# A hybrid decoder step on one core: entry products of 344 columns, the sticks' bias added ahead, w_out loaded early, and a combine that gathers with addition

## The chip, the core and the metric

The kernel is one program on one NeuronCore of a Trainium2 chip. The time is device microseconds from the start to the end of an execution. Five engines work in parallel, each on its own instruction stream: PE (TensorE, matrix products), DVE (VectorE), ACT (ScalarE), POOL (GpSimd) and SP (SyncE, which here only issues transfers). Sixteen DMA engines move data between HBM and the on-chip memory. Products land in eight PSUM banks; everything else on the chip lies in one large SBUF allocation that the kernel calls the arena, beside the activations h (token rows) and hT (transposed).

## The reference

One inference step of a one-layer hybrid trunk, for a prompt of 1024 tokens and a sample group of 8 sequences with 4 tokens each; the model width is 1024, all numbers are float32.

```python
h = layer_norm(x, ln0)
z = h @ w_in                      # split: qa ka va | ub vb | xc | qkv | zg | bd ad
# A stick-breaking attention, 4 heads of 64
z = q @ k.T * dh**-0.5 + bias
log_beta, log_keep = log_sigmoid(z), where(mask, log_sigmoid(-z), 0)
after = exclusive reverse cumulative sum of log_keep over the keys
oa = where(mask, exp(log_beta + after), 0) @ v
# B chunked gated MLP, C causal pooling of windows 2/4/8/16, D gated delta rule in chunks of 64
h = layer_norm(ALPHA * h + concat(oa, ob, oc, od) @ w_out, ln1)
h = layer_norm(ALPHA * h + cross_attention(h, mem_k, mem_v), ln2)   # mem_k = mem_prompt @ xa_wk
# 16 experts in 4 groups, the best two of the best group, gates g1, g2
h = layer_norm(ALPHA * h + g1 * expert1(h) + g2 * expert2(h), ln3)
```

The sample group runs through the same weights with cached keys, values and states. The outputs are the two streams and all new caches and states.

## The kernel before

The program is a row of fourteen stages, each in one block at whose end all engines join. Within a stage each engine runs its instructions in the order in which they are written, and semaphores order the engines against each other. There is no scheduler: the order in the code is the order on the engine. Tokens lie in nine tiles, eight of 128 prompt tokens and one of the 32 sample tokens (`TILES`, `rows(i)`). A float32 product is recorded as two matmul instructions. The places that the change touches:

**Entry** (`stage_entry`, lines 302 to 494). DVE normalises tile after tile, PE transposes it (L455) and multiplies it by the first part of w_in (L471): two products of 512 columns (keys and values; gate values and pooling input) and one of 8 columns (the delta gates), each over eight parts of the depth. ACT copies the four quarters out of the banks, DVE the 8 columns. SP issues the eight x tiles, the weights behind x tile 1, and stores h, k and v per tile.

**Sticks** (`stage_stick_prompt`, 881 to 1078). Eight query blocks of 128; block qb attends to qb+1 key blocks, the diagonal one first: 36 steps. A step n is: scores(n) on PE (L957), add_bias(n) on DVE (L1039), softplus(n) in three activations on ACT (L1009 to L1011), soft_sum(n) on DVE (L1047, and L1050 for the mask on a diagonal), suffix(n) on PE (L967, and L971 off the diagonal), argument(n) on DVE (L1056), weights(n) on ACT (L1017), values(n) on PE (L987). In an iteration n of the loops PE runs scores(n), suffix(n-1), values(n-2); ACT weights(n-2), softplus(n); DVE argument(n-2), soft_sum(n-1), add_bias(n). The waits that matter: add_bias(n) for the four products of scores(n), suffix(n-1) for soft_sum(n-1), argument(n-2) for suffix(n-2).

**Sample** (`stage_sample_and_inputs`, 1081 to 1372): the sample's attention over the cached pages (keys transposed by PE, `turn`, L1165 on), the delta rule's gates and decays (L1178), and the norms of its queries, keys and values, all in one order per engine.

**Delta and residual** (`stage_delta`, 1374 on; `stage_residual`, 2115 on, run twice, for w_out with tag "o" and for xa_wo with tag "w"). SP reloads h in the delta stage and loads w_out at the residual's start in four pieces (L2151). ACT rounds each piece to a high part (L2258), DVE makes the low part (L2231), PE multiplies in three passes (L2110 to L2112), DVE adds to h (L2211).

**Memory** (`stage_memory`, 2283 on): PE transposes mem_prompt (L2326) and multiplies by xa_wk and xa_wv (L2340); SP issues all of it at the stage's start.

**Route and experts** (`stage_route`, 2707 on; `stage_experts`, 2911 on): the route makes for every row of an expert's tile the token that it reads, by one-hot products (L2772). The experts' hidden product is a DVE multiply.

**Combine** (`stage_combine`, 3161 to 3250): POOL gathers the two expert rows of every token into a ring of six buffers (L3193), DVE multiplies each by its gate and adds it to h (L3219) and takes statistics (L283 to L285), ACT normalises (L3250), DVE multiplies by the gain (L3229), POOL adds the shift (L3206), SP stores.

Of the kernel before, what the change touches and what calls it, by code (L numbers as in the profile page):

```python
# [176 lines left out]
def setup(nc, ctx, T, O):  # L177
# [86 lines left out]
    c.gate, c.off = small(2 * TILES), small(2)  # L264
# [37 lines left out]
def stage_entry(c):  # L302
# [28 lines left out]
    w_in, const_in, ln_in = s("e_w"), s("e_const"), s("e_ln")  # L331
    eps_set, stats, rstd_ok, normed = s("e_eps"), s("e_stats"), s("e_rstd"), s("e_normed")
    turned, hT_ok, proj_kv, proj_vx, proj_ba = s("e_turned"), s("e_hT"), s("e_kv"), s("e_vx"), s("e_ba")
    kv_out, vx_out, ba_out, k_turned, kT_ok = s("e_kvo"), s("e_vxo"), s("e_bao"), s("e_kt"), s("e_kTo")
    stored = [s("e_stored0"), s("e_stored1")]
    dve_chain, act_chain, zeroed = s("e_dve"), s("e_act"), s("e_zero")
    w_view = T['w_in'][0].rearrange("(k p) n -> p k n", p=P)

    with nc.Block() as block:
        @block.sync  # L340
        def _(sp):
            for i in range(TILES):
# [11 lines left out]
            for i in range(TILES):  # L354
                sp.wait_ge(normed, i + 1)
                sp.dma_start(c.tokens_dram[i * P:i * P + rows(i), :], h[0:rows(i), i, :]).then_inc(h_out, 16)
                sp.wait_ge(kv_out, 2 * i + 2)
# [13 lines left out]
        def _(dve):  # L371
# [6 lines left out]
            def evac_ba(i):  # L378
                dve.wait_ge(proj_ba, i + 1)
                nc.vector.tensor_copy(c.ba[0:rows(i), i, :], ps[4][0:rows(i), 0:8]).then_inc(ba_out, 1)  # L380

            for i in range(TILES):
# [9 lines left out]
                if i >= 2:  # L392
                    evac_ba(i - 2)
            evac_ba(TILES - 2)
            evac_ba(TILES - 1)

        @block.scalar
        def _(act):
# [6 lines left out]
            def evac(i):  # L405
                r = rows(i)
                act.wait_ge(proj_kv, i + 1)
# [3 lines left out]
                nc.scalar.copy(ktok[0:r, i % 2, :], ps[2 + 4 * (i % 2)][0:r, 0:256]).then_inc(kv_out, 1)  # L411
                nc.scalar.copy(vtok[0:r, i, :], ps[2 + 4 * (i % 2)][0:r, 256:512]).then_inc(kv_out, 1)
                act.wait_ge(proj_vx, i + 1)
                nc.scalar.copy(vg[0:r, i, :], ps[3 + 4 * (i % 2)][0:r, 0:256]).then_inc(vx_out, 1)
                nc.scalar.copy(xc[0:r, i, :], ps[3 + 4 * (i % 2)][0:r, 256:512]).then_inc(vx_out, 1)
# [14 lines left out]
            for i in range(TILES + 2):  # L430
# [8 lines left out]
                if 1 <= i <= TILES:  # L439
# [5 lines left out]
        def _(pe):  # L445
# [13 lines left out]
            def project(i):  # L459
                r = rows(i)  # L460
# [2850 lines left out]
```

## Time and profile before

| | |
|---|---|
| median of 3 runs | 1683.14 us (1682.97 to 1685.85) |
| profiled execution, its span | 1684.2 us, 1682.4 us |
| mean granted clock of TensorE | 0.908 of 2.4 GHz |
| busy: PE, DVE, ACT, POOL | 1386.1, 747.3, 448.1, 207.7 us |
| moved | 174.30 MB, mean 104 GB/s |

The stages by the trace (from join to join, read from busy time per window):

| stage | from, to us | PE busy | DVE | ACT | clock |
|---|---|---|---|---|---|
| entry | 0, 174.8 | 152.1 | 44.0 | 28.8 | 1.00 |
| features, gate and pool | 174.8, 364.0 | 167.7 | 85.4 | 63.1 | 0.94, 0.78 |
| sticks | 364.0, 500.8 | 113.7 | 87.1 | 91.3 | 0.94 |
| sample and inputs | 500.8, 535.5 | 25.1 | 20.9 | 19.6 | 0.85 |
| delta | 535.5, 702.0 | 141.9 | 89.6 | 51.4 | 0.85 |
| residual "o" | 702.0, 827.0 | 108.5 | 82.4 | 30.3 | 0.92 |
| memory | 827.0, 902.7 | 62.7 | 5.5 | 4.4 | 0.88 |
| queries, cross | 902.7, 1112.0 | 193.1 | 45.9 | 61.7 | 0.96, 0.98 |
| residual "w" | 1112.0, 1235.9 | 108.0 | 72.6 | 30.3 | 0.95 |
| route | 1235.9, 1289.4 | 23.5 | 27.8 | 2.9 | 0.66 |
| experts | 1289.4, 1606.8 | 289.8 | 126.2 | 43.0 | 0.96 |
| combine | 1606.8, 1682.4 | 0.0 | 59.9 | 21.4 | 0.50 |

The stages follow one another, so their lengths add up to the span. A busy share says how full an engine is in a stage, not what ends it. The clock column is what the chip granted to TensorE: 1.00 is 2.4 GHz and 0.50 is 1.2 GHz. Profiled time and span differ by the 1.8 us that lie around the span.

### The profile page before, as it was taken

How to read it: one execution, taken by the hardware profiler on the slowest of the kernel's cores; microseconds unless marked ns; L12 is line 12 of the kernel's file. 1: busy time of each engine (PE TensorE's matmuls, PEld its weight loads, DVE VectorE, ACT ScalarE, POOL GpSimd, SP SyncE). 2: the span in 40 equal slices, each digit the busy share in tenths (PEclk: the TensorE clock that was granted, in tenths of full speed). 3: DMA queues.
4: the chain of work that ended last, by engine and by line, in shares of the span. 5: the costliest groups of instructions: out<-in, count | busy, mean ns of one | idle time of the engine just before them, and what ended most of it. 6: DMA issues, size and time to landing. Idle time of an engine off the chain costs nothing. (4 is left out here: it accounts for less than half of the span.)

```text
span 1682.4 us, 24853 instructions
## 1 busy us (share of the span) xinstructions
PE 1386.1 (82%) x9807; PEld 936.7 (56%) x9808; DVE 747.3 (44%) x1132; ACT 448.1 (27%) x928; POOL 207.7 (12%) x196
## 2 busy tenths in 40 slices
PE   4999899778886997699698998969961998999900
PEld 2554799654444787488446987858821333333300
DVE  3321545237655564576401003346535443444368
ACT  1111424236765332322101214431110111111122
POOL 0000000003332751000000000000000110111056
PEclk9999899879997998599798999989985999999955
DMA  8110111022002100300351115430054495772153
GB/s 316 38 57 30 34 49 51 18 76 57 1 1 93 29 4 4 117 22 1 115 185 38 38 50 194 157 133 1 1 237 192 157 360 211 275 295 99 51 220 139
DMA packets 76946, 174.30 MB, mean 104 GB/s; under 512 B 12932, under 2 KB 40715, under 8 KB 70435
## 3 DMA queue, kind: packets, MB, share of 16 engines
q1 hardware_dynamic: 67387, 137.73, 23.2%
q0 software_dynamic: 5856, 21.24, 3.7%
q10 hardware_dynamic: 3600, 13.90, 2.0%
q8 instruction: 73, 1.20, 0.3%
q14 instruction: 30, 0.25, 0.0%
HBM read 142.27 MB, written 30.66 MB: 103 GB/s over the span
## 5 line engine op out<-in xcount | busy, mean ns | idle before, releaser
L2997 PE MATMUL bank<-arena,hT 128*64 x384 | 173.7, 606 | 11.3 <-DVE hT L3106 4.9
L2998 PE MATMUL bank<-arena,hT 128*64 128x512 f32 x384 | 173.7, 606 | 0.0
L471 PE MATMUL bank<-arena,hT 128*128 128x512 f32 (+3 forms) x432 | 141.1, 481 | 0.0
L2997 PEld LDWEIGHTS bank<-arena,hT 128*64 128x64 f32 x384 | 53.5, 140 | 124.2 <-issue 124.2
L3116 DVE COPY arena<-arena 128x4096 f32 x24 | 55.1, 2295 | 131.3 <-PE bank L2998 119.3
L471 PEld LDWEIGHTS bank<-arena,hT 128*128 128x128 f32 (+1 forms) x432 | 68.5, 184 | 72.8 <-issue 72.8
L2965 POOL DMA_INDIRECT hT<-tokens,row_token x24 | 40.3, 1678 | 440.4 <-PE bank L2982 229.8
L2111 PE MATMUL bank<-hT_rest,f_w_high 128*128 128x352 f32 x288 | 93.7, 326 | 0.0
L3021 PE MATMUL bank<-arena,hT 128*64 x192 | 87.5, 598 | 2.4 <-ACT hT L3061 2.4
L3023 PE MATMUL bank<-arena,hT 128*64 128x512 f32 x192 | 87.5, 598 | 0.0
L1577 PE MATMUL bank<-arena 64*64 64x64 f32 (+1 forms) x1920 | 68.6, 224 | 3.5 <-DVE arena L1950 3.0
L1577 PEld LDWEIGHTS bank<-arena 64*64 64x64 f32 x1920 | 64.2, 136 | 11.0 <-issue 6.5
L2110 PE MATMUL bank<-hT_high,q_w_high 128*128 128x352 f32 x192 | 62.6, 326 | 7.6 <-DVE q_w_low L2401 7.6
L2110 PE MATMUL bank<-o_w_high,o_s_high 128*128 128x512 f32 (+1 forms) x144 | 57.6, 400 | 12.6 <-DVE o_w_low L2231 12.6
L2110 PE MATMUL bank<-w_w_high,w_s_high 128*128 128x512 f32 (+1 forms) x144 | 57.5, 399 | 10.6 <-DVE w_w_low L2231 10.6
L2110 PE MATMUL bank<-f_h_high_a,f_w_high 128*128 128x352 f32 x180 | 59.2, 329 | 6.6 <-DVE f_w_low L668 6.6
L3061 ACT COPY hT<-bank 128x256 f32<-128x256 f32 x24 | 8.9, 373 | 204.6 <-PE bank L3009 202.3
L2112 PE MATMUL bank<-hT_high,q_w_low 128*128 128x352 f32 x192 | 63.3, 329 | 0.0
L2111 PE MATMUL bank<-hT_low,q_w_high 128*128 128x352 f32 x192 | 63.0, 328 | 0.0
L967 PE MATMUL bank<-arena,const 128*128 128x512 f32 x72 | 42.7, 677 | 21.4 <-DVE arena L1050 11.8
L2340 PE MATMUL bank<-arena 128*128 128x512 f32 x128 | 57.2, 609 | 2.0 <-DMA arena<-in_xa_wk_dram 2.0
L2112 PE MATMUL bank<-f_h_high_a,f_w_low 128*128 128x352 f32 x180 | 58.8, 327 | 0.0
(484 smaller groups left out, 2979.3 us busy)
## 6 DMA issues: line engine op xcount, KB each, us to landing
arena<-in_ex_wg_dram SPq DMA_DIRECT2D x16, 1024.0 KB, 7.5
arena<-in_ex_wu_dram SPq DMA_DIRECT2D x16, 1024.0 KB, 10.2
arena<-in_ex_wd_dram SPq DMA_DIRECT2D x16, 1024.0 KB, 12.3
expert_rows<-hT ACTq DMA_DIRECT2D x24, 512.0 KB, 5.2
arena<-in_cache_mem_k_dram SPq DMA_DIRECT2D x8, 1024.0 KB, 4.9
arena<-in_w_in_dram SPq DMA_DIRECT2D x12, 512.0 KB, 3.9
h<-in_x_prompt_dram SPq DMA_DIRECT2D x8, 512.0 KB, 8.9
arena<-in_w_in_dram SPq DMA_DIRECT2D x2, 2048.0 KB, 17.1
```

Of the source, the lines that this page charges most:

```text
L471: last = nc.tensor.matmul(ps[bank][0:r, 0:n], hT[:, k, i * P:i * P + r], wt[:, k, col:col + n], start=(k == 0), stop=(k == KC - 1))
L967: last = nc.tensor.matmul(ps[4 + n % 2][:, :], K("negsuf"), sp_[:, n % 3].rearrange(flat), start=True, stop=(kb == qb))
L1577: last = nc.tensor.matmul(out(q, hd), stationary(q, hd), moving(q, hd), start=True, stop=True)
L2110: nc.tensor.matmul(out, high, w_high, start=start, stop=False)
L2111: nc.tensor.matmul(out, high, w_low, start=False, stop=False)
L2112: return nc.tensor.matmul(out, low, w_high, start=False, stop=stop)
L2340: last = nc.tensor.matmul(ps[4 + u % 4][:, :], memT[:, k, m * P:(m + 1) * P], w[:, half % 3, k, :], start=(k == 0), stop=(k == KC - 1))
L2997: nc.tensor.matmul(ps[UPB[u % 2]][0:LR, :], xT[:, u % 2, k, 0:LR], gate_up_of[:, bass.ds(slot, 1), :, k, :].rearrange("p a g f -> p (a g) ...
L2998: last = nc.tensor.matmul(ps[UPB[u % 2]][LR:P, :], xT[:, u % 2, k, LR:P], wB_gate_up[:, :, k, :], start=(k == 0), stop=(k == KC - 1))
L3021: nc.tensor.matmul(ps[DNB[q]][0:LR, :], hidT[:, u % 2, f, 0:LR], down_of[:, bass.ds(slot, 1), f, n].rearrange("p a n -> p (a n)"), start=( ...
L3023: last = nc.tensor.matmul(ps[DNB[q]][LR:P, :], hidT[:, u % 2, f, LR:P], wB_down[:, f, n], start=(f == 0), stop=(f == 1))
L3116: nc.vector.tensor_copy(wB[:, 0:2 * EW], c.xw[:, bass.ds(e & 3, 1), 0:2 * EW].rearrange("p a n -> p (a n)")).then_inc(copied_up, 1)
```

## The change

Six edits, in the order of the program.

Entry: the 1032 columns of the weights are cut into three products of 344 columns instead of 512, 512 and 8. They rotate through five banks. The weights come in these thirds, and the first of them is issued in front of x tile 1. ACT copies the first two thirds, DVE the last. The sample tile is computed as four products of 256 or 264 columns that stand side by side in four groups of 32 columns of the array, and DVE copies all of it.

```diff
+    W3 = 344
+    THIRDS = (((0, KA, W3),), ((W3, KA + W3, 512 - W3), (512, VB, 2 * W3 - 512)), ((2 * W3, VB + 2 * W3 - 512, 1024 - 2 * W3), (1024, BD, 8)))
+    BANKS = (2, 3, 4, 6, 7)
...
-                if i == 1:
-                    sp.dma_start(wt[:, :, 0:512], w_view[:, :, KA:KA + 512]).then_inc(w_in, 16)
-                    sp.dma_start(wt[:, :, 512:1024], w_view[:, :, VB:VB + 512]).then_inc(w_in, 16)
-                    sp.dma_start(wt[:, :, 1024:1032], w_view[:, :, BD:BD + 8]).then_inc(w_in, 16)
+                if i < 2:
+                    for n in ((0,), (1, 2))[i]:
+                        for at, col, w in THIRDS[n]:
+                            sp.dma_start(wt[:, :, at:at + w], w_view[:, :, col:col + w]).then_inc(w_in[n], 16)
...
+                    for k in range(KC):
+                        last = nc.tensor.matmul(bank_of(i, n)[:, 0:W3], hT[:, k, t], wt[:, k, n * W3:(n + 1) * W3],
+                                                start=(k == 0), stop=(k == KC - 1))
+                    last.then_inc(third[n], 1)
+
+            def project_sample():
+                pe.wait_ge(hT_ok, 2 * NT + 2)
+                pe.wait_ge(vg_out, NT - 1)
+                for k in range(KC):
+                    for j in range(4):
+                        n = 264 if j == 3 else 256
+                        last = nc.tensor.matmul(bank_of(NT, 0)[j * NS:(j + 1) * NS, 0:n], hT[:, k, SEQ:TOK],
+                                                wt[:, k, j * 256:j * 256 + n], start=(k == 0), stop=(k == KC - 1))
```

The transfers that SP issues at the program's start, before:

```order
L343 DMA h<-in_x_prompt_dram 128x1024
L345 DMA arena<-in_ln_g_dram 128x1024
L346 DMA arena<-in_ln_b_dram 128x1024
L343 DMA h<-in_x_prompt_dram 128x1024
L348 DMA arena<-in_w_in_dram 128x8x512
L349 DMA arena<-in_w_in_dram 128x8x512
L350 DMA arena<-in_w_in_dram 128x8x8
```

The same place of the changed kernel (x tiles are L349 there, the weights L356):

```order
L349 DMA h<-in_x_prompt_dram 128x1024
L351 DMA arena<-in_ln_g_dram 128x1024
L352 DMA arena<-in_ln_b_dram 128x1024
L356 DMA arena<-in_w_in_dram 128x8x344
L349 DMA h<-in_x_prompt_dram 128x1024
L356 DMA arena<-in_w_in_dram 128x8x168
L356 DMA arena<-in_w_in_dram 128x8x176
L356 DMA arena<-in_w_in_dram 128x8x336
L356 DMA arena<-in_w_in_dram 128x8x8
```

The first 344 columns of the weights have moved in front of the second x tile; the other columns stay behind it.

Sticks: in DVE's loop add_bias(n) stands before argument(n-2) and soft_sum(n-1), and no longer behind them. PE's and ACT's loops are as they were.

```diff
             for n in range(N + 3):
                 if n >= 3 and steps[n - 3][0] == steps[n - 3][1]:
                     mask_weights(n - 3)
+                if n < N:
+                    add_bias(n)
                 if 2 <= n <= N + 1:
                     argument(n - 2)
                 if 1 <= n <= N:
                     soft_sum(n - 1)
-                if n < N:
-                    add_bias(n)
```

DVE in the sticks stage around the end of a query block, before (L1065 copies a block's output, L1061 is the mask on the weights, L1056 argument, L1047 soft_sum, L1039 add_bias):

```order
L1065 COPY hT<-bank 128x2x128 [waits a_pv]
L1061 TENSOR_TENSOR arena<-arena,const 128x512 [waits a_exp]
L1056 TENSOR_TENSOR arena<-bank,arena 128x512 [waits a_sp,a_sums]
L1047 SCALAR_TENSOR_TENSOR arena<-arena 128x512 [waits a_sumok,a_sums,a_soft]
L1039 TENSOR_TENSOR arena<-bank,arena 128x512 [waits a_exp,a_score]
L1056 TENSOR_TENSOR arena<-bank,arena 128x512 [waits a_sp,a_sums]
```

And in the changed kernel (L1102, L1098, L1076 add_bias, L1093 argument, L1084 soft_sum):

```order
L1102 COPY hT<-bank 128x2x128 [waits a_pv]
L1098 TENSOR_TENSOR arena<-arena,const 128x512 [waits a_exp]
L1076 TENSOR_TENSOR arena<-bank,arena 128x512 [waits a_exp,a_score]
L1093 TENSOR_TENSOR arena<-bank,arena 128x512 [waits a_sp,a_sums]
L1084 SCALAR_TENSOR_TENSOR arena<-arena 128x512 [waits a_sumok,a_sums,a_soft]
L1076 TENSOR_TENSOR arena<-bank,arena 128x512 [waits a_exp,a_score]
```

The operation that waits for the scores (a_score) is now the first of a step's three; the other two keep their order.

Sample: PE begins with the first square sums, transposes the keys of all eight sequences in one run, then does the second square sums and the decays (in bank 4 instead of 5); the order of ACT and DVE follows, and one memset goes from DVE to POOL.

```diff
+            square_sums(0)
             pe.wait_ge(c.k_pages_in, 16 * NPAGES)
-            for b in range(4):
+            for b in range(DB):
                 turn(b)
+            square_sums(1)
             decays()
-            for b in range(4, DB):
-                turn(b)
-            square_sums(0)
             pe.wait_ge(q_ok, 3)
```

Delta, residual and memory: the delta stage no longer reloads h; SP loads w_out into h's place there. The residual takes w_out from it, and h's tiles are loaded when the fourth low part is made. At the residual's end, behind the last product, SP issues the memory tensor and the first half of xa_wk.

```diff
-            sp.dma_start(c.h[:, 0:NT, :], c.tokens_dram[0:SEQ, :].rearrange("(i p) d -> p i d", p=P)).then_inc(sx["hin"], 16)
-            sp.dma_start(c.h[0:NS, NT, :], c.tokens_dram[SEQ:TOK, :]).then_inc(sx["hin"], 16)
+            load_w_out(c, sp)
...
+            if split:
+                sp.wait_ge(wl_ok, 4)
+                for i in range(TILES):
+                    sp.dma_start(h[0:rows(i), i, :], c.tokens_dram[i * P:i * P + rows(i), :]).then_inc(h_in[i], 16)
             c.clear_semaphores(sp)
+            if split:
+                sp.wait_ge(prod, 2 * TILES)
+                load_memory_first(c, sp)
...
+def load_w_out(c, sp):
+
+    wv = c.T['w_out'][0].rearrange("(k p) n -> p k n", p=P)
+    raw = c.h[:, 0:KC, :]
+    for n in range(4):
+        sp.dma_start(w_piece(raw, n), w_piece(wv, n)).then_inc(c.w_out_in[n], 16)
```

Route and experts: the one-hot products carry a second set of 24 columns, each entry times the token's gate, so that every row of an expert's tile has its gate (`row_gate`), and the experts' hidden product multiplies by it.

```diff
+                ins = vt.tensor_tensor(x[:, :, 1, :], x[:, :, 1, :],
+                                       c.gate[:, q * TILES:(q + 1) * TILES].unsqueeze(2).to_broadcast([P, TILES, NL]), ALU.mult)
...
+            link(vt.tensor_copy(c.row_gate, ps[3][:, MOE_TILES:2 * MOE_TILES]))
...
-                nc.vector.tensor_tensor(hid[:, u % 2, :], ps[UPB[u % 2]][:, DE:2 * DE], sg[:, u % 2, :], ALU.mult).then_inc(hid_ok, 1)
+                nc.vector.scalar_tensor_tensor(hid[:, u % 2, :], ps[UPB[u % 2]][:, DE:2 * DE], c.row_gate[:, bass.ds(t, 1)],
+                                               sg[:, u % 2, :], ALU.mult, ALU.mult).then_inc(hid_ok, 1)
```

Combine: the first gather of a tile adds its rows into h on the way, the second goes into its own buffer; none waits. DVE adds the second, takes statistics, and applies mean, gain, reciprocal deviation and shift in two instructions. ACT computes the reciprocal deviation only.

```diff
             for i in range(TILES):
-                for n in (S + 2 * i, S + 2 * i + 1):
-                    if n < 2 * TILES:
-                        gather(n)
                 r = rows(i)
-                gp.wait_ge(gained, i + 1)
-                nc.gpsimd.tensor_tensor(h[0:r, i, :], h[0:r, i, :], b[0:r, :], ALU.add).then_inc(normed, 1)
+                gp.indirect_dma_start(h[0:r, i, :], None, expert_rows, rows_of(i, 0), compute_op=ALU.add).then_inc(added[i], 16)
+                gp.indirect_dma_start(second[0:r, i, :], None, expert_rows, rows_of(i, 1)).then_inc(second_in[i], 16)
...
+            def measure(i):
+                r = rows(i)
+                dve.wait_ge(added[i], 16)
+                dve.wait_ge(second_in[i], 16)
+                nc.vector.tensor_tensor(h[0:r, i, :], h[0:r, i, :], second[0:r, i, :], ALU.add).then_inc(summed, 1)
...
+                x = h[0:r, i, :]
+                link(nc.vector.scalar_tensor_tensor(x, x, c.mv[0:r, i % 2, 0:1], g[0:r, :], ALU.subtract, ALU.mult))
+                nc.vector.scalar_tensor_tensor(x, x, c.rstd[0:r, i % 2, :], b[0:r, :], ALU.mult, ALU.add).then_inc(normed, 1)
```

## Rows read from the trace of the kernel before

**Rows 1.** The page's chain that ended last, by line.

```profile
DVE h L3219 2%; DVE h L3229 1%; DMA arena<-expert_rows,slot 0%; DVE small L283 0%; DVE small L284 0%; POOLq L3174 0%; POOL h L3206 0%; DVE small L285 0%; DVEq L3218 0%; PEldq L3174 0%
```

**Rows 2.** Source view, L967: duration ns min/median/max, first and last us, forms.

```profile
L967 PE MATMUL bank<-arena,const x72: 592/697/1220, 371.6 to 496.5; 128*128 128x512 f32 x72
```

**Rows 3.** Timeline, sticks: start us, us, engine line op out<-in xcount [idle <-releaser].

```profile
401.97 1.12 PE L967 MATMUL bank<-arena,const 128*128 128x512 f32 x2
...
402.93 1.02 PE L971 MATMUL bank<-arena,const 128*128 128x512 f32 x2
...
403.88 0.66 PE L987 MATMUL bank<-arena 128*64 128x128 f32 x8
...
403.99 0.69 DVE L1056 TENSOR_TENSOR arena<-bank,arena 128x512 f32<-128x512 f32 x1 [1.36 <-PE bank L971]
...
404.47 0.72 PE L957 MATMUL bank<-arena 64*128 64x128 f32 x8
404.64 0.69 DVE L1047 SCALAR_TENSOR_TENSOR arena<-arena 128x512 f32<-128x512 f32 x1
...
405.26 0.69 DVE L1039 TENSOR_TENSOR arena<-bank,arena 128x512 f32<-128x512 f32 x1
...
405.39 1.12 PE L967 MATMUL bank<-arena,const 128*128 128x512 f32 x2 [0.21 <-DVE arena L1047]
```

**Rows 4.** Lines, sticks stage: busy us, mean ns | idle us before, releaser.

```profile
L1009 ACT ACTIVATE arena<-arena 128x512 f32<-128x512 f32 x36 | 22.7, 630 | 33.8 <-DVE arena L1039 33.8
```

**Rows 5.** Timeline at a diagonal step of the sticks.

```profile
408.74 0.69 DVE L1050 TENSOR_TENSOR arena<-arena,const 128x512 f32<-128x512 f32 x1
...
411.13 0.71 PE L957 MATMUL bank<-arena 64*128 64x128 f32 x8
...
412.05 0.69 DVE L1047 SCALAR_TENSOR_TENSOR arena<-arena 128x512 f32<-128x512 f32 x1 [0.71 <-ACT arena L1011]
...
412.66 0.68 DVE L1039 TENSOR_TENSOR arena<-bank,arena 128x512 f32<-128x512 f32 x1
```

**Rows 6.** Windows: us, busy PE, PEld, DVE, ACT, POOL, PEclk, DMA share, GB/s.

```profile
364.00:380.00 16.00, 9.49 (x44) 5.40 (x44) 8.11 (x15) 8.21 (x12) 1.86 (x3) 0.50 0.46 128
...
564.00:568.00 4.00, 2.46 (x80) 2.31 (x76) 3.35 (x13) 0.21 (x1) 4.00 (x7) 1.00 0.02 6
```

**Rows 7.** Timeline: entry, and the sample's packed products at 518 us.

```profile
12.28 0.70 DVE L283 BATCH_NORM_STATS2 small<-h 128x6 f32<-128x512 f32 x1 [11.07 <-DMA h<-in_x_prompt_dram]
...
43.58 15.58 PE L471 MATMUL bank<-arena,hT 128*128 128x512 f32 x48
...
158.69 14.41 PE L471 MATMUL bank<-arena,hT 128*32 128x512 f32 x48
...
518.28 3.66 PE L1207 MATMUL bank<-arena 128*32 128x256 f32 x64
```

**Rows 8.** Windows, transfers at the start.

```profile
12.00:14.00 2.00, 0.00 (x0) 0.00 (x0) 1.50 (x3) 0.07 (x1) 0.00 (x0) 1.00 1.05 409
```

**Rows 9.** Timeline, sample stage, PE before the decays.

```profile
510.60 0.61 PE L1178 MATMUL bank<-small,const 128*128 128x32 f32 x2 [6.55 <-DVE small L1320]
```

**Rows 10.** Timeline, starts of residual "o" and of memory.

```profile
707.30 1.90 ACT L2258 CAST o_w_high<-arena 128x2048 fp32r<-128x2048 f32 x1 [2.87 <-DMA arena<-in_w_out_dram]
...
832.08 3.67 PE L2326 MATMUL bank<-const,arena 128*128 128x128 f32 x16 [5.82 <-DMA arena<-in_mem_prompt_dram]
...
837.71 29.60 PE L2340 MATMUL bank<-arena 128*128 128x512 f32 x64 [1.96 <-DMA arena<-in_xa_wk_dram]
```

**Rows 11.** Timeline, route.

```profile
1283.25 1.25 DVE L2903 TENSOR_TENSOR arena<-arena 128x432 f32<-128x432 f32 x2
```

**Rows 12.** Timeline, combine: a pair alone, two pairs beside POOL's addition.

```profile
1614.84 2.69 DVE L3219 SCALAR_TENSOR_TENSOR h<-arena,small,h 128x1024 f32<-128x1024 f32 x2 [11.14 <-DMA arena<-expert_rows,slot]
...
1624.21 4.56 DVE L3219 SCALAR_TENSOR_TENSOR h<-arena,small,h 128x1024 f32<-128x1024 f32 x2
...
1631.34 4.56 DVE L3219 SCALAR_TENSOR_TENSOR h<-arena,small,h 128x1024 f32<-128x1024 f32 x2
```

More of the change, by code:

```diff
@@ L405, in evac @@
             def evac(i):
-                r = rows(i)
-                act.wait_ge(proj_kv, i + 1)
+                act.wait_ge(third[0], i + 1)
                 if i >= 2:
@@ L459, in project @@
             def project(i):
-                r = rows(i)
                 pe.wait_ge(hT_ok, 2 * i + 2)
-                for bank, col, n, out_sem, free in ((2 + 4 * (i % 2), 0, 512, proj_kv, kv_out),
-                                                    (3 + 4 * (i % 2), 512, 512, proj_vx, vx_out),
-                                                    (4, 1024, 8, proj_ba, ba_out)):
-                    if bank == 4:
-                        if i >= 1:
-                            pe.wait_ge(free, i)
-                    elif i >= 2:
-                        pe.wait_ge(free, 2 * (i - 1))
-                    for k in range(KC):
-                        last = nc.tensor.matmul(ps[bank][0:r, 0:n], hT[:, k, i * P:i * P + r],
-                                                wt[:, k, col:col + n], start=(k == 0), stop=(k == KC - 1))
-                    last.then_inc(out_sem, 1)
+                t = slice(i * P, (i + 1) * P)
@@ L1300, in _ @@
             nc.vector.tensor_tensor(tx, ad, bc, ALU.add).then_inc(gd, 1)
-            dve.wait_ge(q_ok, 1)
-            for half in range(2):
-                r = slice(half * DH, (half + 1) * DH)
-                nc.vector.tensor_copy(diagonal(qz[r, half:HEADS:2]),
-                                      qT[r, :, SEQ:TOK].rearrange("p c (b q) -> p c b q", b=DB)).then_inc(q_ok, 1)
-            nc.vector.tensor_tensor(sq[:, 0], qkvT[:, 0, :], qkvT[:, 0, :], ALU.mult).then_inc(sq_ok[0], 1)
             def turned_keys(b):
@@ L1378, in stage_delta @@
     nc, T, O, K = c.nc, c.T, c.O, c.K
+    c.w_out_in = [c.sem(f"w_out{n}") for n in range(4)]
     PAIRS = NT // 2
@@ L2128, in stage_residual @@
     s = lambda n: c.sem(f"{tag}_{n}")
-    w_in = [s(f"w{n}") for n in range(4)]
+    if split:
+        place_memory(c)
+        c.mem_in, c.half_in = s("mem"), [s(f"half{n}") for n in range(3)]
+    w_in = c.w_out_in if split else [s(f"w{n}") for n in range(4)]
+    raw = h[:, 0:KC, :] if split else w
+    h_in = [s(f"h{n}") for n in range(TILES)] if split else []
     ln_in, prod, added, stats, rstd_ok, normed, turned, hT_ok, low_ok = (
@@ L2149, in _ @@
         def _(sp):
-            for n in range(4):
-                sp.dma_start(piece(w, n), piece(wv, n)).then_inc(w_in[n], 16)
+            if not split:
+                for n in range(4):
+                    sp.dma_start(w_piece(w, n), w_piece(wv, n)).then_inc(w_in[n], 16)
             sp.dma_start(g, row_bc(T[gain][0])).then_inc(ln_in, 16)
@@ L2257, in _ @@
                 act.wait_ge(w_in[n], 16)
[L2258 removed]
+                nc.scalar.copy(w_piece(wh, n), w_piece(raw, n)).then_inc(wh_ok, 1)
             src_high(1)
@@ L2305, in _ @@
         def _(sp):
-            sp.dma_start(mem, T['mem_prompt'][0].rearrange("(m p) n -> p m n", p=P)).then_inc(mem_in, 16)
-            for n in range(4):
+            for n in range(1, 4):
                 if n == 3:
```

263 lines of the change are left out of this document (143 added, 120 removed).

## The prediction

> **What bounds the kernel now.** I read the page's chain of waits first. It followed only the last stage back [rows 1]: the chain stops at the join of all engines at a stage's end, so it says that the combine is bound by DVE's multiply-adds and nothing of the thirteen stages before. The stages follow one another, so a change is priced stage by stage. The table of stages (busy time of each engine between the joins) shows PE as the fullest engine in all but the route and the combine, with two kinds of gap: PE waiting for a transfer at a stage's start, and DVE alone in the combine. For the stages touched I read the timeline.
>
> The stage that matters most is the sticks. The suffix sums of its 36 steps run from 371.6 to 496.5 us [rows 2]. One full step [rows 3]: PE multiplies the suffix sums (L967, L971), the values (L987) and the next scores (L957), 3.22 us from the start of L967 at 401.97 to the end of the scores at 405.19; then 0.20 of gap, and the next L967 starts at 405.39. The period is 3.42 us. DVE does its three operations meanwhile: argument(n-2) (L1056) as soon as L971 has ended, soft_sum(n-1) (L1047) behind it, add_bias(n) (L1039) last. It is not full, it waited 1.36 us for L971. ACT is not full either: it waited 33.8 us in 36 steps for add_bias [rows 4]. So the longest path now is suffix sum, argument, soft_sum, suffix sum: values and scores lie beside the two DVE operations and cost almost nothing.
>
> **The sticks, changed.** DVE's order becomes add_bias(n), argument(n-2), soft_sum(n-1); PE's stays: scores(n), suffix(n-1), values(n-2). Nothing is removed; one instruction is moved past two. add_bias(n) waits for scores(n), the last thing PE does before suffix(n-1), and suffix(n-1) waits for soft_sum(n-1), now behind add_bias(n) in DVE's queue. Does a DVE instruction that could run overtake one that waits? At the diagonal the scores had ended at 411.13+0.71 = 411.84, yet add_bias started at 412.66, behind a soft_sum that itself waited for ACT until 412.05 [rows 5]. It does not overtake.
>
> By the Trainium skill ("PSUM — Partial Sum Buffer", section "Engine vs sequencer instructions") ScalarE's, VectorE's and GpSimdE's queues are strictly first in, first out, and TensorE's products start in program order. The trace agrees by the 0.82 us of rows 5. Were the rule wrong here, the change would give the small gain that I price below as the third rival.
>
> So the step is a ring in which nothing overlaps: PE 3.22; from the end of the scores to add_bias 0.04 (as from L971's end, 403.95, to L1056 at 403.99); add_bias to argument 0.65 (403.99 to 404.64 is the same step between two such operations); argument to soft_sum 0.65; start of soft_sum to start of L967 0.75 (404.64 to 405.39). Sum 5.31, against 3.42: +1.89 [rows 3]. Steps differ at the diagonals of the eight query blocks. Before a diagonal block's suffix sum DVE multiplies once more by the mask, L1050 at 0.69 [rows 5], say 6.0; behind it there is no L971, 0.95 less, 4.3. The 35 intervals between suffix sums: 6 of 6.0, 6 of 4.3, 20 of 5.3, and at the two ends 4.4, 4.3 and 3.4: 36.0+25.8+106.0+12.1 = 179.9. The same count with the old order gives 124.5 where the trace has 124.3 (371.6 to the start of the last pair), so the recurrence is sound. **+55.** Low end: operations of 0.62 back to back with no hand-over, 1.9 of gap less what the easy steps hide, some +1.3 a step, +45. High end: what TensorE's clock does in the new gaps. From 364 to 380 us PE was busy 9.5 of 16 and its clock 0.50, which is 1.2 GHz; from 564 to 568 it was busy 2.46 of 4, as full as it will be here (3.2 of 5.3), and the clock stayed 1.00, 2.4 GHz [rows 6]. I take the second; at the lower level a step costs 3.2 more, and six such steps make +75, the high end.
>
> **Entry.** A prompt tile has 48 PE instructions, 32 of them of 512 columns and 16 of 8, in 15.58 us; the sample tile's 48, with a quarter of the weights' columns, take 14.41 [rows 7]. Were the narrow ones free, one of 512 would take 14.41/32 = 0.45; they are not, and at 0.04 each it is 0.43. One of 344 then takes 0.43x344/512 = 0.289 and a tile 48x0.289 = 13.9 (14.5 from the 0.45): 8x1.7 = -13.6. The sample tile becomes 32 products of 256 or 264 columns, four side by side in groups of 32 columns of the array. The form is in the trace: 64 instructions of 256 columns, 128x32 weights, in 3.66 [rows 7]. 14.41 down to 3.66: -10.8. At the end DVE must copy five pieces and the stores wait for all of them, 3.2 us where 1.65 stood: +1.6. At the start SP issues the first third of the weights, 1.41 MB, ahead of x tile 1; DVE's first statistics wait for tiles 0 and 1 (12.28) and at 409 GB/s [rows 7, 8] that is +3.6. The two copies of the third part that go from ACT to DVE (0.4 each) and the bank rotation lie beside PE, which was busy 152 of the stage's 175 us. Sum **-19.2**; -23 if the start is hidden, -12 if PE runs at 14.8 a tile (0.45 an instruction of 512, and a hand-over between banks).
>
> **Sample stage.** PE idled 6.55 before the decays [rows 9], because DVE and ACT came late with the gates; the new order puts the keys' transposes and two square sums there. The tail of the stage (softmax of the sample, 10 us of short DVE and ACT steps) stays. Half is likely given back where ACT's first norms now stand before the keys: **-2** (-5 to +3).
>
> **w_out early.** In the residual ACT waited 2.87 for the first quarter, and PE's first product stood behind it: -2.8. h is now loaded again tile by tile once the last low part is made. DVE turns to the second half of the sources' low part first (1.2 us) and then to tile 0's first addition, which may wait some 1 us for the transfer; PE's products go on into other banks meanwhile, so I cost this at nothing, 1.3 if that cover is gone. The memory tensor and the first half of xa_wk are issued before the residual's end: PE's 5.82 and 1.96 [rows 10] go, less about 1 for PE starting at the lower clock. **-2.8** and **-6.5** (-5 to -8).
>
> **Route and experts.** Two more DVE multiplies of half-size, 1.25 for the pair like L2903's [rows 11], a copy, and one-hot products of 48 columns instead of 24: **+2** (+1.5 to +3.5). The gate enters the hidden multiply as a third operand; DVE idles half of that stage: 0.
>
> **Combine.** The pair of multiply-adds took 4.56 wherever POOL's addition ran beside it, 2.69 where none did, and a tile took 7.13 (1624.21 to 1631.34) [rows 12]. Now the first gather adds into h, DVE adds the second (1.3 at most), takes statistics (1.4) and applies gain and shift with two multiply-adds (2.7): 5.3 a tile, 47.7 for nine. POOL does only gathers. From 1616.1 that ends at 1663.8 where POOL's last addition ended at 1680.0: -16; I take **-15**. How long an accumulating gather takes no row shows. The plain one landed within 7.3 us of its issue; if accumulating is no dearer than 1.5 times that, it stays beside DVE. End for a dear one: five times a plain gather's 1.24, 6.2+1.2 = 7.4 a tile, no gain or +5. Range -18 to +5.
>
> The Trainium skill ("DMA: Bandwidth & Descriptors", section "Rules for kernel authors") says that an accumulating DMA reads its destination and writes it later. By an estimate from that, three streams of bytes instead of two make 1.9 us out of 1.24 and the -15 holds. No run here shows it.
>
> **The sum.** -19.2 +55 -2 -2.8 -6.5 +2 -15 = +11.5 on the profiled execution's 1684.2: **1695** us. That execution is 1.1 above the median of the runs shown; I leave this in.
>
> **Rivals.**
> - TensorE's clock falls in the sticks' new gaps. For it: the first 16 us of the stage at 0.50; against: the 564 to 568 row. With half of the steps at the lower level +56 more: 1750.
> - The accumulating gather is slow. No row speaks against it. Combine +0 to +5: about 1712.
> - The sticks are not slowed and the change is faster. This would need add_bias's wait to be covered: DVE has 1.36 us of wait a step, and if the moved operation fills that and PE's scores come early enough, the period stays PE's 3.2 to 3.3 us. The sum is then -43.5-5: 1636. Against: scores(n) is directly in front of suffix(n-1) on PE, rows 3. With 1.3 us of the 1.89 covered, 1657. The deciding point is (43.5)/35 = 1.24 us a step: less than that and the kernel is faster.
> - The gains come out larger and the loss smaller, each at its end: 45-23-18-5-2.8-8+1.5 = -10, or they cancel, near 1680.
>
> **Chances and range.** Forecast 0.63; clock 0.08; gather 0.12; sticks not slowed 0.07; cancelling 0.10. Range 1674 to 1720: it takes in the cancelling case and the slow gather and leaves out the clock and the fast sticks with some of the tails. A measurement of this kernel tells 0.2%, 3.4 us, from no change. Slower: the forecast, clock and gather cases less their tails, 0.79. Within 0.2%: most of the cancelling case and a little tail, 0.08. Faster: 0.13.
>
> **What the changed profile would show.** Sticks: L1084 (soft_sum) behind L1076 (add_bias) that waits for PE's scores some 2 us a step, PE idle 2.1 before each suffix sum ended by DVE's soft_sum, ACT's waits up, period 5.3. Wrong if PE's gap there is under 1.2. The clock column of 380 to 550 us shows the first rival. Entry: 13.9 a prompt tile, first product near 28.8. Memory: first transpose less than 1.5 us after the join. Combine: no POOL additions, tiles 5.3 apart, DVE waiting for the gathers in h if the second rival holds. The forecast fails mainly if the new order of DVE does not stop PE.

## The result, and the profile after

The changed kernel takes 1752.07 us in the median of 4 runs (1749.47 to 1752.58), against 1684.35 for the kernel before: a ratio of 1.0399, interval 1.0381 to 1.0417. It is slower, as forecast, but by 68 us and not by 11.5.

The stages, from join to join, in the profiled executions (the changed one has a span of 1750.6):

| stage | before | after | difference | the prediction's term |
|---|---|---|---|---|
| entry | 174.8 | 156.1 | -18.7 | -19.2 |
| features, gate and pool | 189.2 | 188.0 | -1.2 | 0 |
| sticks | 136.8 | 246.9 | **+110.1** | **+55** |
| sample and inputs | 34.8 | 33.8 | -1.0 | -2 |
| delta | 166.5 | 166.0 | -0.5 | 0 |
| residual "o" | 125.1 | 123.0 | -2.1 | -2.8 |
| memory | 75.6 | 69.6 | -6.0 | -6.5 |
| queries, cross, residual "w" | 333.2 | 335.1 | +1.9 | 0 |
| route | 53.4 | 54.1 | +0.7 | +2 |
| experts | 317.6 | 316.6 | -1.0 | 0 |
| combine | 75.5 | 61.5 | -14.0 | -15 |

Without the sticks the sum is -41.9, forecast -43.5. Of the error of 56.7 us (68.2 against 11.5 in the spans) 55.1 lie in one stage. From the page of the changed kernel, the engines and two groups (line engine op, names, shapes, count | busy us, mean ns of one | idle before, releaser):

```profile
PE 1413.6 (81%) x9823; PEld 965.3 (55%) x9824; DVE 740.6 (42%) x1154; ACT 425.8 (24%) x897; POOL 186.9 (11%) x188
...
L1004 PE MATMUL bank<-arena,const 128*128 128x512 f32 x72 | 69.3, 1062 | 79.9 <-DVE arena L1084 55.2
...
L1076 DVE TENSOR_TENSOR arena<-bank,arena 128x512 f32<-128x512 f32 x36 | 24.8, 691 | 146.0 <-PE bank L994 145.9
```

L1004 is the first suffix product (L967 before), L1076 add_bias, L1084 soft_sum. Two things are to be seen. PE stood 79.9 us ahead of its suffix products, waiting for DVE (55.2 for soft_sum, the rest for the mask on the diagonals), and DVE stood 146 us ahead of add_bias, waiting for PE: they take turns, as forecast. And a product of L1004 takes 1062 ns in the mean, where L967 took 677 (median 697 [rows 2]), though the product itself is unchanged. One step in the timeline, a full one as in [rows 3] though of a later query block (start us, us, engine line op):

```profile
424.37 2.07 PE L1004 MATMUL bank<-arena,const 128*128 128x512 f32 x2 [2.02 <-DVE arena L1084]
...
426.23 1.60 PE L1008 MATMUL bank<-arena,const 128*128 128x512 f32 x2
427.77 0.66 PE L1024 MATMUL bank<-arena 128*64 128x128 f32 x8
428.36 0.72 PE L994 MATMUL bank<-arena 64*128 64x128 f32 x8
429.14 0.69 DVE L1076 TENSOR_TENSOR arena<-bank,arena 128x512 f32<-128x512 f32 x1 [2.88 <-PE bank L994]
429.75 0.68 DVE L1093 TENSOR_TENSOR arena<-bank,arena 128x512 f32<-128x512 f32 x1
430.35 0.68 DVE L1084 SCALAR_TENSOR_TENSOR arena<-arena 128x512 f32<-128x512 f32 x1
```

The scores end at 429.08, add_bias starts 0.06 later, argument 0.61, soft_sum 0.60 after that, and the next suffix product follows. PE's gap ahead of L1004 is 2.02: the ring and its DVE part are those of the prediction (2.09). But PE's own part is longer: L1004's pair takes 2.07 instead of 1.12 and L1008's 1.60 instead of 1.02. The windows of the stage show why (us, busy PE, PEld, DVE, ACT, POOL, PEclk, DMA share, GB/s), first the changed kernel behind its first 36 us, then the kernel before:

```profile
380.00:580.00 200.00, 137.09 (x588) 62.90 (x586) 69.06 (x105) 70.16 (x117) 33.58 (x29) 0.72 0.00 0
```

```profile
400.00:496.00 96.00, 84.89 (x543) 42.64 (x541) 62.90 (x96) 69.32 (x111) 31.70 (x27) 1.00 0.00 1
```

The granted clock was 0.72 over 200 us where it had been 1.00. It is a mean of two levels. In the step above L1004 runs at 1.2 GHz, directly behind the gap, and L1024 and L994 at 2.4 GHz (0.66 and 0.72, as before); in the step ahead of it L1024 took 1.12. One full step of this kernel ran at 2.4 GHz throughout, the very place of [rows 3]:

```profile
405.30 1.12 PE L1004 MATMUL bank<-arena,const 128*128 128x512 f32 x2 [2.02 <-DVE arena L1084]
...
410.53 2.08 PE L1004 MATMUL bank<-arena,const 128*128 128x512 f32 x2 [2.01 <-DVE arena L1084]
...
420.07 1.12 PE L1024 MATMUL bank<-arena 128*64 128x128 f32 x8
```

From 405.30 to 410.53 it took 5.23 us, where the prediction had 5.31. The other full steps took 6.6 to 6.8.

The entry answers to [rows 7]:

```profile
16.33 0.69 DVE L283 BATCH_NORM_STATS2 small<-h 128x6 f32<-128x512 f32 x1 [15.12 <-DMA h<-in_x_prompt_dram]
...
29.24 15.14 PE L498 MATMUL bank<-arena,hT 128*128 128x344 f32 x48
...
45.09 14.05 PE L498 MATMUL bank<-arena,hT 128*128 128x344 f32 x48
...
149.06 3.77 PE L508 MATMUL bank<-arena,hT 128*32 128x256 f32 x64
```

A prompt tile takes 14.05 (forecast 13.9), the sample tile 3.77 (3.66), and the first statistics start at 16.33, 4.05 later than before (3.6). The memory stage answers to [rows 10]:

```profile
913.78 3.65 PE L2390 MATMUL bank<-const,arena 128*128 128x128 f32 x16 [0.95 <-PEq L2203]
...
918.10 4.50 PE L2404 MATMUL bank<-arena 128*128 128x512 f32 x5 [0.68 <-ACT arena L2416]
```

PE's first transposes waited for nothing but the join, and the first half of xa_wk was there. In the residual ACT no longer waited for w_out, but DVE's first addition waited 2.28 us for h's first tile:

```profile
807.25 0.69 DVE L2277 SCALAR_TENSOR_TENSOR h<-h,bank 128x512 f32<-128x512 f32 x1 [2.28 <-DMA h<-tokens]
811.12 0.69 DVE L2277 SCALAR_TENSOR_TENSOR h<-h,bank 128x512 f32<-128x512 f32 x1 [3.18 <-PE bank L2141]
```

The next addition waited 3.18 for PE: DVE's wait was off the path. The combine answers to [rows 12]:

```profile
1700.55 1.22 DVE L3273 TENSOR_TENSOR h<-h,arena 128x1024 f32<-128x1024 f32 x1 [14.72 <-DMA arena<-expert_rows,slot]
...
1709.46 1.22 DVE L3273 TENSOR_TENSOR h<-h,arena 128x1024 f32<-128x1024 f32 x1
...
1714.64 1.22 DVE L3273 TENSOR_TENSOR h<-h,arena 128x1024 f32<-128x1024 f32 x1
```

A tile takes 5.18 us from 1709.46 on, but DVE starts 11.5 us into the stage, where it was 7.9 before and the prediction had 9.2. POOL's issue of an accumulating gather takes longer and the gathers land later (source view of the accumulating one: duration ns min/median/max, first and last start; then issue to landing, us min/median/max):

```profile
L3262 POOL DMA_INDIRECT h<-expert_rows,slot x9: 1541/1549/2082, 1689.8 to 1717.7; - x9
...
DMA to landing us min/median/max: 9.4/11.6/14.7
```

The plain gathers that stand between them (L3263) land as late, 8.8/11.9/15.2 us, and it is such a one that DVE's first addition waited for.

### The profile page after: what moved, and what is told of

Read it like the earlier page. It is cut to its first block and busy times, and to the rows that moved or that the text cites. A ratio compares the mean times of both kernels' runs of the same rounds, so it can differ in the third digit from the quotient of the medians.

```text
span 1750.6 us, 24935 instructions
## 1 busy us (share of the span) xinstructions
PE 1413.6 (81%) x9823; PEld 965.3 (55%) x9824; DVE 740.6 (42%) x1154; ACT 425.8 (24%) x897; POOL 186.9 (11%) x188
## 5 line engine op out<-in xcount | busy, mean ns | idle before, releaser
L1004 PE MATMUL bank<-arena,const 128*128 128x512 f32 x72 | 69.3, 1062 | 79.9 <-DVE arena L1084 55.2
L498 PE MATMUL bank<-arena,hT 128*128 128x344 f32 x384 | 113.6, 456 | 0.0
L3185 DVE COPY arena<-arena 128x4096 f32 x24 | 55.1, 2295 | 130.4 <-PE bank L3066 118.3
L498 PEld LDWEIGHTS bank<-arena,hT 128*128 128x128 f32 x384 | 73.0, 192 | 37.0 <-issue 0.9
L1076 DVE TENSOR_TENSOR arena<-bank,arena 128x512 f32<-128x512 f32 x36 | 24.8, 691 | 146.0 <-PE bank L994 145.9
L1004 PEld LDWEIGHTS bank<-arena,const 128*128 128x128 f32 x72 | 16.6, 287 | 87.8 <-DVE arena L1084 61.3
L1054 ACT ACTIVATE arena<-arena 128x512 f32<-128x512 f32 x36 | 22.7, 630 | 152.1 <-DVE arena L1093 152.1
```

Of the source, the lines that this page charges most:

```text
L498: last = nc.tensor.matmul(bank_of(i, n)[:, 0:W3], hT[:, k, t], wt[:, k, n * W3:(n + 1) * W3], start=(k == 0), stop=(k == KC - 1))
L1004: last = nc.tensor.matmul(ps[4 + n % 2][:, :], K("negsuf"), sp_[:, n % 3].rearrange(flat), start=True, stop=(kb == qb))
L3185: nc.vector.tensor_copy(wB[:, 0:2 * EW], c.xw[:, bass.ds(e & 3, 1), 0:2 * EW].rearrange("p a n -> p (a n)")).then_inc(copied_up, 1)
```

## The experiments

All times are medians of at least 4 runs; the kernel before ran beside each at 1682.3 to 1683.2.

**The order undone.** The changed kernel with DVE's order in the sticks as before.

```diff
-                if n < N:
-                    add_bias(n)
                 if 2 <= n <= N + 1:
                     argument(n - 2)
                 if 1 <= n <= N:
                     soft_sum(n - 1)
+                if n < N:
+                    add_bias(n)
```

> The changed kernel with one edit undone: in the sticks DVE runs argument(n-2), soft_sum(n-1), add_bias(n) again. Theory (the order alone costs the sticks' 110 us, the other edits gain): the sticks return to 136.8 us with the clock near 1.00 behind the first 16 us, and the whole is 1752-110 = about 1642, some 42 below the kernel before. Rival (the loss in the sticks comes in part from the other edits, such as what the entry leaves in the banks or a clock that stays low after the earlier stages): the sticks stay above 145 us and the whole above 1650.

Measured: 1643.54 us, ratio to before 0.9759 (0.9743 to 0.9776). The sticks take 136.7 us, and from 380 to 480 the clock is 1.00:

```profile
380.00:480.00 100.00, 88.03 (x562) 44.14 (x560) 63.69 (x97) 70.11 (x112) 33.02 (x29) 1.00 0.00 1
```

The theory holds: one moved instruction costs all that the sticks lost, and the other five edits gain 40 us together. Of these five only the early loads, the first gather's addition and the place of the first third of the weights are undone by themselves below; what the others give is read from their stages in the table.

**The order alone.** The same edit the other way round, in the kernel before.

> The kernel before with one edit done: add_bias(n) ahead of argument(n-2) and soft_sum(n-1) on DVE in the sticks. Theory: +110 us, 1793, all of it in the sticks, with a period of 6.7 us and a granted clock near 0.7 there. By the recurrence of the prediction without any fall of the clock: +55, 1738. Rival (the loss needs the other edits): less than +20.

Measured: 1792.48 us, ratio 1.0649 (1.0631 to 1.0667), +109. The sticks take 248.4 us, with the clock at 0.71:

```profile
400.00:600.00 200.00, 137.57 (x587) 62.51 (x586) 68.22 (x103) 69.88 (x116) 33.53 (x29) 0.71 0.00 0
```

The loss does not depend on the other edits.

**The gap filled.** The changed kernel with four idle products behind each step's scores.

```diff
+            def filler(n):
+                if n >= 1:
+                    pe.wait_ge(zb_ok, n)
+                for q in range(4):
+                    nc.tensor.matmul(ps[2 * ((n + 1) % 2) + q % 2][:, 0:2 * P], kT[:, 0, 0:P], qT[:, 0, 0:2 * P],
+                                     start=True, stop=True)
+
             for n in range(N + 2):
                 if n < N:
                     scores(n)
+                    filler(n)
```

> The changed kernel with four further PE products of 128x256 float32 behind each step's scores, written to the two score banks of the other parity, which DVE has read a step before; nothing uses them. They take some 1.7 us at 2.4 GHz and so fill most of the 2.1 us in which PE waits for DVE's three operations. Theory (the ring of three DVE operations costs +55 and TensorE's lower clock the other +55): the clock goes back to about 1.00 in the sticks, the period falls from 6.7 to 5.3 us although PE has more to do, the stage from 247 to about 190 and the whole to about 1695. Rival (PE's slow products come from something other than its gaps, such as bank or port contention with DVE): nothing of that, the period is 6.7 plus 0 to 1.7, the whole 1752 or more.

Measured: 1704.37 us, ratio 1.0126 (1.0103 to 1.0149). PE does 144 more products than the changed kernel and the whole is 48 us faster. In the profiled execution the cross-attention stage, where nothing was changed, took 118.1 us at a clock of 0.93 (111.6 and 0.98 in the changed kernel), so the sticks gave more than the whole shows. The sticks take 192.3 us. The source view of the first suffix product and a window:

```profile
L1004 PE MATMUL bank<-arena,const x72: 592/645/697, 352.5 to 532.2; 128*128 128x512 f32 x72
```

```profile
380.00:530.00 150.00, 143.69 (x790) 85.77 (x788) 68.00 (x102) 69.67 (x116) 33.65 (x29) 1.00 0.00 1
```

No suffix product took more than 697 ns. PE still waits for DVE, but only 0.09 us ahead of a full step's suffix product. With the clock at 1.00 the ring takes 179.2 us from the start of the first pair of suffix products to that of the last (the 532.2 above is the second product of the last pair), where the prediction's recurrence has 179.9. So the +110 is two terms: +55.5 (192.3 against 136.8) for the ring, and +54.6 (246.9 against 192.3) for the clock. The cut between them is not quite clean: 5.9 of the 54.6 lie in the first three intervals (20.8 us without the idle products, 14.9 with them), where the kernel before ran at 0.50 too; the products raised the clock of the first 16 us to 0.80. The rival, that the products were slow for another reason than the gaps, falls: DVE's three operations and the banks that they read are the same here.

**Half the gap filled.** As above with `range(2)`.

> The changed kernel with two idle products behind each step's scores instead of four, 1.0 us of PE's gap of 2.1. With four the clock was 1.00 and the stage 192 us, with none it was about 0.72 and 247. Theory A (what the clock grants goes step by step with how full PE is): the clock lies between, some 0.85 to 0.95, the stage at 200 to 225 us. Theory B (the remaining gap of 1.1 us is as harmless as the one with four): the clock is 1.00 and the stage 192 us again, the whole 1704.

Measured: 1698.71 us, ratio 1.0095 (1.0071 to 1.0119); the sticks 194.4 us.

```profile
380.00:530.00 150.00, 118.71 (x667) 63.89 (x668) 67.95 (x102) 68.55 (x114) 32.79 (x29) 0.99 0.00 1
```

Theory B in the main: PE's gap ahead of a full step's suffix product was 0.95 us, 1.68 on the diagonals, and the clock was 0.99, with a few products at 1.2 GHz behind one of the diagonals' gaps (0.91 from 420 to 440). In the changed kernel the gaps were 2.0 and 2.7, and it was 0.72. The whole came 5.7 us below the theory's 1704; in the two profiled executions the sticks are 2.0 longer here and the cross-attention stage, 111.6 us, is 6.5 shorter.

**The scores ahead on PE too.** The changed kernel, and PE issues the scores one step earlier.

```diff
+            scores(0)
             for n in range(N + 2):
-                if n < N:
-                    scores(n)
+                if n + 1 < N:
+                    scores(n + 1)
                 if 1 <= n <= N:
                     suffix(n - 1)
```

> The changed kernel, DVE's order as changed, but PE runs scores(n+1) instead of scores(n) ahead of suffix(n-1), so add_bias(n) finds its scores made a step before. Theory (the order is bad only because the scores come directly ahead of the suffix sum): add_bias goes into DVE's wait for the suffix sum; the recurrence gives 114.5 us from first to last suffix sum where the old order has 123.3 and the changed one 177.0 at full clock, so the sticks take about 128 us and the whole about 1633, 8 below the kernel with the old order. Rival (ACT's softplus or DVE is the next bound and the step stays at 3.4 us): the same as with the old order, 1642.

Measured: 1634.60 us, ratio 0.9723 (0.9706 to 0.974), the lowest of all medians here. The same DVE order that costs 110 us is harmless as soon as the scores are not directly ahead of the suffix sum. The sticks take 132.2 us (forecast 128). One step:

```profile
413.24 1.12 PE L1004 MATMUL bank<-arena,const 128*128 128x512 f32 x2
413.32 1.27 POOL L980 TENSOR_TENSOR arena<-arena 128x512 f32<-128x512 f32 x1 [2.09 <-DVE arena L1085]
413.35 0.69 DVE L1077 TENSOR_TENSOR arena<-bank,arena 128x512 f32<-128x512 f32 x1 [0.17 <-ACT arena L1055]
...
414.20 1.02 PE L1008 MATMUL bank<-arena,const 128*128 128x512 f32 x2
...
415.26 0.69 DVE L1094 TENSOR_TENSOR arena<-bank,arena 128x512 f32<-128x512 f32 x1 [1.22 <-PE bank L1008]
```

add_bias (L1077) now runs beside PE's L1004, in the time in which DVE waited before; argument (L1094) still waits for L1008, so a full step is 3.36 (409.88 to 413.24), hardly less than 3.42. There the rival was right. The gain lies in the two steps behind a diagonal, 2.51 and 3.76 us where the old order took 3.3 and 3.4. The suffix sums take 119.7 us from first to last, where the theory had 114.5 and the old order measures 124.2. So the 1634.6 met the forecast 1633 in part by luck: the sticks gave 4.4 of the 10.0 us between the two profiled executions (1642.1 and 1632.1), and the rest came from stages that are the same in both kernels, 2.2 of it in the memory stage.

**Both orders alone**, in the kernel before.

> The kernel before with two edits in the sticks and nothing else: add_bias(n) ahead on DVE and scores(n+1) ahead on PE. Theory (the pair is a gain by itself, as 132.2 against 136.7 us of the stage in the two kernels with all other edits): the sticks are some 4.5 us shorter and the whole 1678 to 1679. Rival (the 4.5 us came from the clock at the start of the stage): 1681 to 1685.

Measured over 10 runs: 1681.26 us (1677.28 to 1684.32), ratio 0.9987 (0.9972 to 1.0002). The interval includes 1: the gain of the pair is not shown by the time. The sticks are 133.7 us, 3.1 less than before. In three further traces with both orders they took 133.2 to 134.3. Of the 4.5 us in the expectation 1.5 came from the first three steps of that one execution, where the clock was 0.66 in the first 16 us and 0.51 in this one; so far the rival holds.

**A plain gather.** In the combine the first gather without its addition.

```diff
-                gp.indirect_dma_start(h[0:r, i, :], None, expert_rows, rows_of(i, 0), compute_op=ALU.add).then_inc(added[i], 16)
+                gp.indirect_dma_start(h[0:r, i, :], None, expert_rows, rows_of(i, 0)).then_inc(added[i], 16)
```

> The kernel with the scores ahead, and the first gather of each combine tile overwrites h instead of adding into it, so the scaled h is missing from the last sum (left out for the measurement). In the changed kernel POOL's issue of an accumulating gather takes 1.55 us where a plain one took 0.94, the landings take 9.4 to 14.7 us, and DVE waits till 11.5 us after the stage's start. Theory A (the accumulate costs issue time and landing time): POOL's first gathers take 0.94 again, DVE's first addition starts some 3 us earlier, and the combine takes 58 to 59 us instead of 61.4. Theory B (the longer issue and landing come from eighteen gathers issued without a pause, plain or not): the combine stays within 1 us.

Measured: 1636.88 us. The combine takes 58.3 us against 60.7 with the scores ahead: theory A, though DVE's first addition starts only 1.3 us earlier (9.30 against 10.55 us into the stage), where the theory had some 3. The whole is not shorter than with the scores ahead (1634.60); the stages from the sticks to the memory took 7.8 us more in this execution, though nothing in them differs.

```profile
L3263 POOL DMA_INDIRECT h<-expert_rows,slot x9: 933/938/1012, 1577.7 to 1599.3; - x9
...
DMA to landing us min/median/max: 6.4/7.4/7.9
```

An accumulating gather costs 0.6 us more of POOL's issue time and lands some 4 us later (11.2 with the scores ahead); the plain gathers behind it land late too. That reaches the end of the stage once, as 2.4 us: DVE waits longer for the first tile, and once more, 0.98 us, for the second. Behind these two tiles DVE, at 5.2 us a tile, is slower than the gathers.

**x tile 1 first.**

```diff
-                if i < 2:
-                    for n in ((0,), (1, 2))[i]:
+                if i == 1:
+                    for n in range(3):
```

> The kernel with the scores ahead, and in the entry x tile 1 is issued ahead of the first third of the weights, as in the kernel before. The prediction priced the third ahead of x tile 1 at +3.6 us for DVE's first statistics. Theory: DVE starts at 12.3 us and the stage is 2 to 4 us shorter, since PE, once it runs, never waits. Rival: PE's first product then waits for the third itself, and the stage stays within 1 us.

Measured: 1634.88 us. DVE's first statistics start at 13.14 instead of 16.41, and the entry is 3.7 us shorter (153.5 against 157.2), as the theory has it. The later stages give as much back in this execution, the sticks 2.0 of it (with the clock at 0.50 over their first 16 us where it was 0.66) and the sample stage 1.1; without this edit the plain-gather kernel has the same two lengths, so they do not come from it. On the whole kernel nothing can be told from the scores-ahead form.

**The early loads undone.** w_out loaded at the residual's start, the memory tensor and the first half of xa_wk at the memory stage's.

```diff
-            load_w_out(c, sp)
             sp.wait_ge(sx["mem"], 1)
...
             if not split:
...
+            else:
+                load_w_out(c, sp)
...
-            if split:
-                sp.wait_ge(prod, 2 * TILES)
-                load_memory_first(c, sp)
...
         def _(sp):
+            load_memory_first(c, sp)
```

> The kernel with the scores ahead, but w_out is loaded into h's place at the residual's start instead of in the delta stage, and the memory tensor and the first half of xa_wk at the memory stage's start instead of the residual's end. Theory (both early loads pay what the waits of the kernel before showed): the residual is 2.9 us longer and the memory stage 5 to 7 longer, together +8 to +10 us, 1643. Rival (the waits come back elsewhere, such as in h's reload): less than +4.

Measured: 1645.57 us, 11 above the form with the early loads; residual and memory take 200.0 us together against 189.6. PE waits 5.9 us for the memory tensor again, ACT up to 2.9 for w_out. The theory holds, but the 10.4 us of these two stages are the high end: the 189.6 held a memory stage of 67.5 us, and five other traces with the early loads have 192.2 to 193.0, which makes 7 to 8.

## Why the prediction was wrong

The direction, the place and the mechanism of the ring, in which PE and DVE take turns, were right. The step that failed is the sentence on TensorE's clock in the term of the sticks: "I take the second; at the lower level a step costs 3.2 more, and six such steps make +75, the high end." The prediction let at most six steps run at the lower level; with a gap of 2.0 us or more ahead of nearly every suffix product the mean clock was 0.72 over 200 us, the first suffix product took 0.98 to 1.22 us instead of 0.70 in 30 of 36 steps, and this cost 54.6 us more. The rival "TensorE's clock falls in the sticks' new gaps" had +56 and 1750 us; it is what happened, and it had a chance of 0.08 and lay outside the range. That its number fits so well is in part luck: it let half of the steps cost 3.2 us more each, while in the trace nearly every step cost some 1.5 more, because only a part of PE's work in it was slow (5.23 against 6.8). Nor does a step that is all at the lower level cost 3.2 more. By an estimate from the changed kernel's trace (L1004, L1008 and L1024 take 1.86, 1.85 and 1.05 us there until the next group starts, the scores 1.23) PE's work in it is 6.0 us instead of 3.22, so 2.8 more.

What misled was the evidence taken for it. The row from 564 to 568 us in [rows 6] (2.46 of 4 us busy, clock 1.00) is one short pause in a full stretch. The windows beside it, and a longer stretch with several waits, two of them of 2.2 and 2.7 us, were in the same trace:

```profile
560.00:564.00 4.00, 4.00 (x132) 3.69 (x130) 2.90 (x8) 2.92 (x9) 4.00 (x7) 1.00 0.03 8
...
568.00:572.00 4.00, 3.85 (x124) 3.70 (x123) 2.33 (x7) 1.15 (x4) 1.92 (x4) 1.00 0.00 0
```

```profile
536.00:556.00 20.00, 13.88 (x143) 8.81 (x142) 6.74 (x18) 6.51 (x17) 16.47 (x21) 0.66 0.76 238
```

A single pause between two full windows did not foretell what the same pause does in every step. The 20 us from 536, the sample stage (25.1 of 34.7 busy, 0.85) and the route (0.66) all ran below the full clock, and the table of stages ahead of the prediction had the last two. None of them repeats one gap in every step as the changed sticks do, so the trace of before could raise the chance of the rival but not show it.

The other steps:
- The ring: PE 3.22 and DVE 2.09, 179.9 us. Shown by the filled gap, 179.2, and by the one step at full clock, 5.23 for 5.31.
- DVE's queue does not overtake. Shown: DVE stood 146 us ahead of add_bias with argument ready behind it.
- Entry, -19.2: measured -18.7. Eight tiles gave 1.5 each rather than 1.7, the start cost 4 instead of 3.6; the first tile gained more (15.14 against 17.50). In the six other traces with this entry and the third ahead of x tile 1 it took 155.4 to 157.2, so -17.6 to -19.4.
- Sample -2: measured -1.0, but no gain is shown: with the new order the stage took 33.8 to 36.3 us in eight traces, with the old one 34.5 to 35.2 in three. w_out -2.8: -2.1; memory -6.5: -6.0. Undoing both loads cost 7 to 10 us in these stages, 9.3 by the forecast.
- Route +2: +0.7 here, up to +1.7 in the other traces. A one-hot product of 48 columns is no dearer than one of 24, 72 in 4.08 against 4.05 us. What was added is two DVE multiplies of 0.61 and a copy of 0.18.
- Combine -15: -14.0. DVE took 5.2 a tile where 5.3 was forecast, and its start came 2.3 us later than forecast. By the plain gather 1.3 us of that belong to the accumulation.
- The rival "the sticks are not slowed" is refuted for this PE order and true for the other one: its condition, that PE's scores come early enough, is just what the scores-ahead kernel makes, and that kernel took 1634.6 where the rival had 1636 (with 4.6 us off the sticks where the rival had 5).

The 1.9 us in the stages from the queries to residual "w" lie in residual "w" (123.4 before, 125.1 after), and there the granted clock was 0.93 where it had been 0.95. Stages that are the same in two kernels differ by 1 to 7 us in this way, with the clock: the memory stage by 2 and the cross-attention stage by 6.5. A difference of a few us in one stage of one trace is therefore not an effect of an edit by itself. What moves the clock in such a stage from execution to execution is not settled.

## What to carry to other kernels

In-order queues make a ring out of two engines as soon as the instruction that waits for the other engine's last work stands ahead of the one that the other engine waits for next; move the producer forward first, then the consumer. Price a new gap of PE twice: once as the gap, and once as PE's own work at the lower clock (here 1.9 and 1.5 us a step), and judge the second by stretches of a trace with the same repeated pattern; a single pause inside a busy stretch misled here. Where no trace has the pattern, one run of the moved instruction alone measures it. Where five edits gain and one loses, a table of stages finds the one.

## What the runs showed of the hardware

- With a gap of 2.0 us in every step of 6.7 to 6.8 us the granted clock was 0.72 over 200 us; two idle products a step, which left a gap of 0.95, brought 0.99, and four, which left 0.09, brought 1.00. Adding useless work to PE made the kernel 48 to 53 us faster.
- An indirect gather that adds into SBUF occupied POOL for 1.55 us against 0.94, and landed in 11.6 us (median) against 7.4; the plain gathers between them landed in 11.9 against 7.3.
- Products of 128x48 took the same time as products of 128x24 (4.08 and 4.05 us for 72 instructions, at a granted clock of 0.50 in both traces); the loads of their 64 weight columns were busy 3.92 us of that in both.
